# Attention outputs made with features on partitions: values stationary, probabilities scaled on ScalarE, products split at their eviction

## What is computed

```python
p = jax.nn.softmax(s + bias[None], axis=-1)                 # branch a, 8 heads of 64
o = jnp.einsum('brjhqk,brjkhd->brjqhd', p.astype(v.dtype), vg)
...
e = jnp.exp(s - m)                                           # branch b, 8 heads, 2 for keys and values
p = e / (jnp.sum(e, axis=-1, keepdims=True) + jnp.exp(sk - m))
o = jnp.einsum('bnkgqs,bnskd->bnqkgd', p.astype(v.dtype), vw)
...
y = (jax.nn.sigmoid(g_a) * jnp.einsum('bte,ed->btd', o_a, w_branch_a[l])
     + jax.nn.sigmoid(g_b) * jnp.einsum('bte,ed->btd', o_b, w_branch_b[l]))
x = x + jnp.einsum('btd,de->bte', y, w_out[l])
```

## Time and profile before

| what | value |
|---|---|
| median of 3 runs | 1025.3 us (1023.84 to 1026.19) |
| span of the profiled execution, first to last instruction | 1023.7 us |
| mean granted TensorE clock | 0.963 |
| TensorE busy | 900.0 us (88%) |
| VectorE busy | 450.4 us (44%) |
| ScalarE busy | 333.2 us (33%) |
| attention loop, first scores to last weighted product | 67.44 to 142.85 us |

### The profile page before, as it was taken

The page is one execution under the profiler, slowest core; times in us unless marked ns, Lnnn a source line. Parts: engine busy times, 40 slices in busy tenths (PEclk is TensorE's granted clock), DMA queues, the critical chain, the costliest instruction groups (busy, mean ns, idle before and its releaser), DMA issues.

```text
span 1023.7 us, 17037 instructions
## 1 busy us (share of the span) xinstructions
PE 900.0 (88%) x7354; PEld 616.5 (60%) x7354; DVE 450.4 (44%) x573; ACT 333.2 (33%) x435; POOL 17.6 (2%) x34
## 2 busy tenths in 40 slices
PE   9999999999999999999999997867778686776865
PEld 8889988888888889989989532212213131221312
DVE  6587778688777348895776310000001000000102
ACT  5456664565455328644433300000000000000002
POOL 1400000000000000000000000000000000000000
PEclk9999999999999999999999999889989899899988
DMA  9984425576645454442359999999999999999994
GB/s 334 238 302 150 166 84 165 165 247 211 197 165 209 161 200 171 165 167 84 114 178 340 392 420 421 421 422 420 422 421 421 424 421 421 424 420 421 421 420 186
DMA packets 87307, 295.01 MB, mean 288 GB/s; under 512 B 6336, under 2 KB 33744, under 8 KB 63809
## 3 DMA queue, kind: packets, MB, share of 16 engines
q1 hardware_dynamic: 81712, 283.92, 71.8%
q10 hardware_dynamic: 3984, 6.34, 1.7%
q0 software_dynamic: 1536, 3.68, 1.3%
HBM read 290.77 MB, written 4.10 MB: 288 GB/s over the span
## 4 chain that ended last, share of the span: by engine, by line
PE 59%; DMA 31%; DVE 5%; SPq 3%; issue 1%; ACT 1%; DVEq 0%; ACTq 0%
DMA arena<-in_w_down 13%; DMA arena<-in_w_up 13%; PE psum L1240 8%; PE psum L1109 6%; PE psum L1111 5%; PE psum L1110 5%; DMA arena<-in_w_gate 5%; PE psum L1919 4%; PE psum L1267 4%; PE psum L1242 4%; PE psum L1605 3%; SPq L909 3%; PE psum L1947 2%; PE psum L1070 1%; PE psum L1146 1%; PE psum L1145 1%
## 5 line engine op out<-in xcount | busy, mean ns | idle before, releaser
L1919 PE MATMUL psum<-arena,featL 128*32 128x512 f32 x1008 | 175.3, 674 | 62.0 <-DMA arena<-in_w_up 46.7
L2457 DVE TENSOR_TENSOR ring_rounded<-arena,hi_rounded 128x2048 fp32r<-128x2048 f32 x77 | 175.9, 2290 | 66.7 <-ACT hi_rounded L2036 65.4
L2036 ACT ACTIVATE hi_rounded<-arena 128x2048 fp32r<-128x2048 f32 x77 | 146.7, 1912 | 95.4 <-DMA arena<-in_w_in 19.1
L1919 PEld LDWEIGHTS psum<-arena,featL 128*32 128x32 f32 x1008 | 39.1, 121 | 185.8 <-DMA arena<-in_w_up 85.3
L1240 PE MATMUL psum<-ffn_in_rounded,hi_rounded 128*128 128x512 f32 x352 | 122.4, 394 | 0.7 <-DVE ffn_in_rounded L2449 0.7
L1947 PE MATMUL psum<-arena,featT 128*32 128x512 f32 x424 | 80.8, 700 | 33.7 <-DMA arena<-in_w_down 29.6
L1109 PE MATMUL psum<-hi_rounded,featT_rounded 128*128 128x256 f32 (+1 forms) x336 | 104.1, 310 | 1.2 <-DVE ring_rounded L2457 0.7
L1111 PE MATMUL psum<-hi_rounded,featL_rounded 128*128 128x256 f32 (+1 forms) x336 | 101.8, 303 | 0.0
L1110 PE MATMUL psum<-ring_rounded,featT_rounded 128*128 128x256 f32 (+1 forms) x336 | 101.8, 303 | 0.0
L1242 PE MATMUL psum<-ffn_in_rounded,ring_rounded 128*128 128x256 f32 x352 | 97.5, 277 | 0.0
L2978 DVE TENSOR_TENSOR featT<-featT,psum 128x512 f32<-128x512 f32 x8 | 8.2, 1031 | 199.9 <-PE psum L1919 199.9
(11 more groups left out here) (348 smaller groups left out, 1323.6 us busy)
## 6 DMA issues: line engine op xcount, KB each, us to landing
arena<-in_w_up SPq DMA_DIRECT2D x73, 1024.0 KB, 26.6
arena<-in_w_gate SPq DMA_DIRECT2D x70, 1024.0 KB, 26.5
arena<-in_w_down SPq DMA_DIRECT2D x61, 1024.0 KB, 26.8
arena<-in_w_in SPq DMA_DIRECT2D x14, 2048.0 KB, 7.9
arena<-in_w_down SPq DMA_DIRECT2D x5, 2048.0 KB, 7.6
arena<-in_w_out SPq DMA_DIRECT2D x3, 2048.0 KB, 8.8
arena<-in_w_in SPq DMA_DIRECT2D x4, 1024.0 KB, 9.1
arena<-in_w_gate SPq DMA_DIRECT2D x12, 256.0 KB, 3.4
```

What stands on the lines that cost most here:

```text
L1919: ins = mm(psum[32 * j:32 * j + 32, MB[4 + m], :], xg[:, 4 * half + k, 32 * j:32 * j + 32], held(place(q, j), j, 512 * k), start=half == 0 ...
L2036: fn(high, view, ACT.Copy).then_inc(hi_ready, 1)
L2457: tt(low, view, high.bitcast(F32), ALU.subtract).then_inc(lo_ready, 1)
```

## The change

The product with the values is made the other way round: the values are the stationary operand (64 columns, so 64 rows of the output, features) and the turned probabilities move through (128 or 256 columns, queries). The two parities write the two halves of the output's partitions. In branch b both pairs of a parity have the same values and go in one matmul. As queries now lie along the free axis of the product, the probabilities are divided by their sums before they are turned: VectorE adds up and inverts the sums right behind `low_part` (`totals`), and ScalarE multiplies the probabilities in place (four activations of 128x256 with a column of `st` as scale). The turned probabilities wait for that instead of for the exponentials. The product is evicted in two halves: ScalarE copies and rounds it into `heads_hi`, VectorE writes the rest to `heads_lo`. `turn_out` and its evictions go. The new tensors lie in `xn`, `rt` and a part of `cst`.

```diff
@@ plan_fills
-        if i == 8:
-            for key in ((0, 0), (0, 1), (1, 0)):
-                add("dve", "oT", *key)
...
-        if br == 1:
-            add("dve", "oT", 1, 1)
@@ TensorE
-            def turn_out(br, t):
-                transposes(("oT", br, t), [xn[:, t, 512 * br + P * k:512 * br + P * (k + 1)] for k in range(4)],
-                           lambda: wait_emptied(pe, "PV", 4 * br + 2 * t + 1))
...
-                    pe.wait_ge(exp_ready, 2 * i + par + 1)
+                    pe.wait_ge(prob_ready, 2 * i + par + 1)
...
-                for h in range(4):
+                out_ = b[:, 0:T].rearrange("p (a q) -> p a q", a=2)
+                for pairs in (slice(0, 2),) if br else (slice(0, 1), slice(1, 2)):
                     for kt in range(NT):
-                        v0 = 2176 + 64 * g if br else 1024 + 64 * (4 * g + h)
-                        ins = mm_halves(b[:, 64 * h:64 * h + 64], probT[:, 2 * (i % 2) + h % 2, h // 2, kt, :],
-                                        nat[:, kt, v0:v0 + 64], kt == 0, kt == NT - 1)
+                        for par in range(2):
+                            v0 = 2176 + 64 * g if br else 1024 + 64 * (4 * g + 2 * pairs.start + par)
+                            ins = mm(out_[64 * par:64 * par + 64, pairs, :], nat[:, kt, v0:v0 + 64],
+                                     probT[:, 2 * (i % 2) + par, pairs, kt, :], start=kt == 0, stop=kt == NT - 1,
+                                     skip_group_check=True)
...
-                if i == 8:
-                    for key in ((0, 0), (0, 1), (1, 0)):
-                        turn_out(*key)
                 if i >= 1:
                     weighted(i - 1)
...
-                        wait_emptied(pe, "oT", br, t)
+                        wait_emptied(pe, "PV", 4 * br + 2 * t + 1)
                         for k in range(4):
-                            ins = mm3(b, [f[:, 4 * br + k, t * P:(t + 1) * P] for f in (featR, featLR)],
+                            ins = mm3(b, [f[br][:, k, t * P:(t + 1) * P] for f in (heads_hi, heads_lo)],
@@ ScalarE, behind the exponentials of iteration i
+                    act.wait_ge(total_ready, i + 1)
+                    for par in range(2):
+                        for pair in range(2):
+                            k = 4 * i + 2 * par + pair
+                            pr = prob[:, i % 2, par, pair, :]
+                            ins = fn(pr, pr, ACT.Copy, scale=sums[:, k:k + 1])
+                            if pair == 0:
+                                a.link(ins)
+                        ins.then_inc(prob_ready, 1)
                     u, c = 5 + i // 2, i % 2
                     wait_filled(act, "p1", u, c)
                     ins = fn(sig[:, :, 256 * i:256 * i + 256], bank("p1", u, c).rearrange("p (t n) -> p t n", t=NT), ACT.Copy)
                     empty(ins, "p1", u, c)
                     if i == 0:
                         qk_moved("qb", "kb")
+                if i >= 1:
+                    br, t, g = (i - 1) // 4, (i - 1) // 2 % 2, (i - 1) % 2
+                    wait_filled(act, "PV", i - 1)
+                    fn(heads_hi[br][:, 2 * g:2 * g + 2, t * P:(t + 1) * P],
+                       bank("PV", i - 1)[:, 0:T].rearrange("p (a q) -> p a q", a=2), ACT.Copy).then_inc(heads_hi_ready, 1)
+                if i < 8:
                     high_part(first["p1", 5] + i + 2)
-            for key in ((0, 0), (0, 1), (1, 0)):
-                high_moved("oT", *key)
             gates(0)
...
-            high_moved("oT", 1, 1)
             gates(1)
@@ VectorE
                 wait_filled(dve, "PT", i, 1)
                 empty(nc.vector.tensor_copy(probT[:, 2 * (i % 2) + 1].rearrange("p a k q -> p (a k q)"), bank("PT", i, 1)),
                       "PT", i, 1)
...
+                dve.wait_ge(heads_hi_ready, i + 1)
+                high, low = (p[br][:, 2 * g:2 * g + 2, t * P:(t + 1) * P] for p in (heads_hi, heads_lo))
+                empty(tt(low, bank("PV", i)[:, 0:T].rearrange("p (a q) -> p a q", a=2), high.bitcast(F32), ALU.subtract), "PV", i)
+
+            def totals(i):
                 s = sums[:, 4 * i:4 * i + 4]
                 dve.wait_ge(exp_ready, 2 * i + 2)
-                if br:
+                if i >= 4:
                     link(tt(s, s, esink[:, 4 * i:4 * i + 4], ALU.add))
-                link(nc.vector.reciprocal(s, s))
-                wait_filled(dve, "PV", i)
...
+                nc.vector.reciprocal(s, s).then_inc(total_ready, 1)
...
                     low_part(first["p1", 5] + i + 1)
+                    totals(i)
                 if i >= 1:
                     weighted(i - 1)
```

More of the change, by code:

```diff
@@ L368, in build @@
         x = sb("x", [P, NT, D])
-        xn = sb("xn", [P, NT, D])
+        xn, xn_r = sb_rounded("xn", [P, NT, D])
         featT, featR = sb_rounded("featT", [P, DK, T])
         featL, featLR = sb_rounded("featL", [P, DK, T])
-        cst = sb("cst", [P, HELD["end"]])
+        cst, cst_r = sb_rounded("cst", [P, HELD["end"]])
         lora, gup, sig_g = (cst[:, slice(*HELD[n])] for n in ("lora", "gup", "gate"))
@@ L379, in build @@
         st = sb("st", [P, 256])
-        rt = sb("rt", [P, 1024])
+        rt, rt_r = sb_rounded("rt", [P, 1024])
         cnt = sb("cnt", [P, 2], I32)
@@ L431, in build @@
         t5w = arena[0:33, L1["biasB"][0] + 1024:L1["biasB"][0] + 1024 + P]
+        heads_hi = (xn_r[:, 0, :].rearrange("p (k q) -> p k q", k=4), rt_r[:].rearrange("p (k q) -> p k q", k=4))
+        heads_lo = (xn_r[:, 1, :].rearrange("p (k q) -> p k q", k=4),
+                    cst_r[:, HELD["lora"][0]:HELD["gup"][1]].rearrange("p (k q) -> p k q", k=4))
         hTh, hTl = (area(LF, n, FFK, T) for n in ("hTh", "hTl"))
@@ L553, in build @@
         exp_ready = sem("exp_ready")
+        total_ready = sem("total_ready")
+        prob_ready = sem("prob_ready")
+        heads_hi_ready = sem("heads_hi_ready")
         gates_ready = sem("gates_ready")
@@ L1395, in _ @@
             for br in range(2):
-                if br == 1:
-                    turn_out(1, 1)
                 for n in range(2):
@@ L1465, in _ @@
                 if c == RW_ORDER[0]:
-                    row_unit(c, 8, 16)
+                    row_unit(c, 8, 12)
                 else:
@@ L2120, in high_moved @@
             def high_moved(*key):
-                h, t = key[1:] if key[0] == "oT" else (key[2], key[1])
+                t, h = key[1:]
                 wait_filled(act, *key)
@@ L2582, in _ @@
                 if br == 1:
-                    low_moved("oT", 1, 1)
                     low_part(first["br", 0] + 3)
```

6 lines of the change are left out of this document (removed).

## The result

| | before | changed |
|---|---|---|
| median, in the same session (4 runs each) | 1024.7 us | 1035.2 us (1032.8 to 1040.2) |
| ratio, 95% interval | | 1.0109 (1.0093 to 1.0125) |
| a second session (5 runs of the changed kernel) | 1024.3 us | 1033.2 us, ratio 1.0087 (1.0072 to 1.0101) |
| span of the profiled execution | 1023.7 us | 1038.3 us; in the second session 1031.4 us |
| attention: first scores to last W | 67.44 to 142.85 us | 67.26 to 150.3 us |

The change is slower by 8.9 to 10.4 us, as forecast (+9.1). Of this 7.3 us arise in the attention, 1.8 less than forecast, and the rest in a later stage, where I had put nothing. The profiled execution of the first session was the slowest of its four (1040.2 us); that of the second session (1033.3 us) lies at its median.

A forecast was written before the change was run, and what follows sets the result against it. TensorE was taken to bound the kernel up to about 540 us, the DMA engines being full only late. Terms 4.3 + 3.8 + 1.5 - 0.4 = 9.1 us gave 1034.4 us on the median of 1025.3; 8-in-10 range 1030.5 to 1037.5.

The forecast's parts named there:

- First iteration, +4.3: Iteration 0: ScalarE's queued wait for totals delays queries and keys; W(0), the first weighted product, starts 4.3 us later.
- TensorE waits about 2 us at W(0): Sign in the profile after: W(0) near 88 us, with TensorE waiting about 2 us for VectorE's copy.
- Nor does a stall bring the clock down: TensorE's clock: where this trace has a stall, the clock stays full (1.00).
- Loop, +3.8: Six W-to-W intervals: a ring through VectorE and ScalarE paces them, 9.08 us in branch a, 10.05 in b; 58.4 against 54.62.
- W left at 1.08: Weighted product on TensorE: still 1.08 us from start to next start; bounds 0.9 and 1.75.
- rival of passes that don't overlap (1.75): Weighted product: long passes on the two output halves don't overlap, W takes 1.75 us, total 1036.5; chance 0.07.
- End of the loop, +1.5: W(7) waits for ScalarE, 4.92 us behind W(6); branch products 6.00 behind W(6) instead of 4.50: +1.5 us.
- Between the branches, -0.44: Four transposes of 0.11 us dropped from TensorE between the branches: -0.44 us.
- All that follows about 9.1 later: After the attention: branch products start near 152.3 instead of 142.8, and everything behind comes about 9.1 us later.
- shorter ring (+7.3): Attention loop: scalings take 0.4 us each with little waiting, so the sum falls to +7.3 (+5.8 at 1.45); chance 0.10.
- Nearly no change: Later stages: their slack takes up the delay, total within 2 us; chance 0.04.
- Faster: Attention: TensorE stays pacemaker if four scalings take under some 1.0 us and don't queue ahead of keys; 1022 us; chance 0.03.

The follow-up runs named there:

- experiment 2: Changed kernel with iteration 0's totals on VectorE moved ahead of the low part; 1032.8 us, 1.0075 of before.
- experiment 4: Changed kernel with the high part moved ahead of the product copy in ScalarE's queue, in each iteration; 1048.9 us, 1.0242 of before.
- experiment 3: Changed kernel with both halves of the product's eviction on VectorE, without ScalarE's product copy; 1032.3 us, 1.0077 of before.
- experiment 6: Changed kernel with iteration 0's totals earlier, both eviction halves on VectorE, and ScalarE's copy for W(7) ahead of its last high part; 1029.1 us, 1.0045.
- experiment 1: Changed kernel without ScalarE's four scalings and its wait for the totals, so probabilities stay undivided; 1027.6 us, 1.0038 of before.
- GpSimd's slow first multiplication: Experiment 6's kernel with one GpSimd multiplication replacing ScalarE's four scalings: 1030.2 us; with totals also behind VectorE's copy: 1028.6 us.
- the padded kernel before: Kernel before the change with 24 matmuls of 8 columns (96 instructions) added ahead of W(7); 1029.4 us, 1.0047 of before.

## Why the prediction held, point by point

- **First iteration, +4.3.** Measured 3.6 (83.66 to 87.29), 3.8 counted from S(0). The mechanism was as described: queries and keys wait behind the scaling. I had the scaling at 76.88 and 1.97 to its successor; it came at 76.59, 0.2 of which is the earlier S(0), and took 1.90. The wait of TensorE's transposes is 1.01 + 0.71, not 2.1. Moving one reciprocal took away 2.2 of it (experiment 2).
- **TensorE waits about 2 us at W(0).** Not in the changed kernel: there the projection ran for 3.4 us at 1.2 GHz and ended just before VectorE's copy did. "Nor does a stall bring the clock down" was read from waits of 0.2 us and applied to ones of 1.0; behind those the clock fell in five of the six executions that had them at this place, and didn't in experiment 4. It cost nothing here, since the fall lay under the wait for VectorE: in experiment 4 the same stretch ran at full clock, and from the first transposes to W(0) it took 9.49 us, here 9.51.
- **Loop, +3.8.** Measured 57.37 us for six intervals against 54.62, +2.75: two of 8.91 (9.08 predicted) and four of 9.89 (10.05). The order of the ring, who waits, and ScalarE's product copy right behind the gate copy were as written. The scaling began 0.07 us earlier in the step (6.44, not 6.51) and gave way after 1.89, not 1.97: together the 0.16 of each step. This was the term of the sum that was most oversized, by 1.05 us. That the ring is the cause in branch b: experiments 1, 3 and 4. In branch a it cost nothing, 8.91 us as before (8.87 with the ring open); the whole +2.75 is branch b's.
- **W left at 1.08.** 1.01 to 1.02, in both forms. The rival of passes that don't overlap (1.75) is out. The Trainium skill's swap (TensorEngine Tiling (Array Packing), Performance Considerations) gave 0.07 us in each W, not a factor: the old form already used both halves.
- **End of the loop, +1.5.** Measured 5.59 from W(6) to the branch products against 4.50, +1.1; W(7) 4.58 behind W(6), not 4.92. Its wait is for the copy that stands behind the high part; experiment 6 moved it and W(7) came at 3.05.
- **Between the branches, -0.44.** Measured -0.2: from the first branch product to the turn 19.46 us instead of 19.66 (142.78 to 162.44). The four transposes go, but not all their time.
- **"All that follows about 9.1 later."** 7.3 later up to 494.6 us. The step that failed is the silent one: I gave the later stages the delay and no change of their own. The stage from 494.6 us took 84.4 to 92.8 instead of 83.1: 1 to 3 us because 352 instructions fewer stand ahead of it, and 6.4 by one execution's fall of the clock. The last part gave back 0.9 to 2.4, which the prediction had named as a sign of being wrong, and which the stage before it outweighed. The two errors, 1.8 too much in the attention and, by the medians, 1.6 to 3.1 too little behind it, nearly cancel: that the total came so near 1034.4 is luck, its direction and its main terms are not. The sum's rounded terms give 9.2, not 9.1; unrounded they give 9.1.
- **The rivals.** The shorter ring (+7.3) is what the attention alone did, by many small amounts rather than by shorter scalings. "Nearly no change" fell: the last part took up 0.9 to 2.4 us, the stage before it lost as much or more. "Faster" fell by its own condition: the four scalings take 1.9 us, not under 1.0, and iteration 0 does queue them ahead of the keys. The remark that free scaling would leave +3.9 was too dark: without scaling and wait only 0.9 remained in the attention (experiment 1), since the wait for the totals goes with it.

What stays open: what sets the length of TensorE's gaps at the ends of blocks, and why most ends have none; why the clock stayed low for 17 us in one execution and not in others with the same gaps; GpSimd's slow first multiplication. That a version with the scaling neither on the ring nor on VectorE's own path would beat the kernel before wasn't found and isn't excluded.

## What to carry to other kernels

Moving a normalisation from behind a product to ahead of it moves it from slack onto the chain that feeds the product: walk the ring from one softmax start to the next through every engine's queue before making the product itself cheaper. A new wait in an in-order queue costs what stands behind it; ask where the first iteration's one-time work stands, and put the wait's producer (here one reciprocal of 0.17 us) ahead of the long operation beside it. Where a change of half a per cent is judged by its total, compare also a stage that it doesn't touch, since a different number of instructions ahead moved such a stage by 1 to 3 us in the profiles: its gaps could lie only at every 256th instruction.

## What the runs showed of the hardware

- The warm-up's form mattered. With 60 matmuls of 64 columns for 30 of 128, everything up to S(0) came 18.9 us later. TensorE's timeline of that kernel:

```profile
1.16 25.86 PE L1077 MATMUL psum<-late 128*128 128x64 f32 x120 [1.16 <-DVE late L2492]
26.82 1.06 PE L1071 MATMUL psum<-cst,xn 128*128 128x128 f32 x4
27.67 2.34 PE L1077 MATMUL psum<-late 128*128 128x128 f32 x10
```

  and of the kernel before, where the 60 records of 128 columns take 9.00 us:

```profile
1.16 9.00 PE L1076 MATMUL psum<-late 128*128 128x128 f32 x60 [1.16 <-DVE late L2485]
9.99 0.60 PE L1070 MATMUL psum<-cst,xn 128*128 128x128 f32 x4
10.43 1.28 PE L1076 MATMUL psum<-late 128*128 128x128 f32 x10
```

  In that kernel the records start 0.213 us apart up to 31.0 us, those of 64 columns and those of 128 alike, so the narrow ones were no cheaper. In the kernel before they start 0.213 us apart up to 5.5 us and 0.111 us apart from there. The trace's first record of the clock, at 2.4 GHz, begins at 31.00 us in the one and at 5.45 in the other; the half pace ahead of it points to 1.2 GHz. A window ahead of that record prints a granted clock of 1.00, because there is no record and not because the clock was full. Why the clock rose so late in this kernel no run takes apart. Taking the 18.9 us off, the kernel is at 1032.8, where the other changed kernels are.
- The same moment explains why S(0) varies without an edit. In the 13 other executions the first record of the clock begins between 4.41 and 7.32 us, and S(0) lies between 66.95 and 68.35, in the same order but for two that differ by 0.01: 1.40 us for 2.91 us more at the slower pace.
- A matmul of 8 columns, its two records and weight loads with it, took 0.12 us (24 in 2.91): cheap filling for a wait, not free beside one.
- Ahead of the experts' part, falls to 1.2 GHz, most of 3.4 us and one each of 6.8, 10.2 and 17.1, came behind waits or gaps of TensorE (0.3 to 1.3 us, in experiment 4 up to 2.8; in the padded kernel before, behind the 24 small matmuls), in some executions and not in others with the same waits. One of 3.4 us cost half its length where TensorE paced (1.7 in the padded kernel before), about a third in the later stage, and nothing where it lay under a wait for another engine.
